# Three value projections in other column blocks, in a decoder of two blocks on one core

## The chip, the cores and the metric

The kernel runs on one core of one Trainium2 chip. The metric is the device time of one execution in microseconds (us), as the median over runs; lower is better.

The core has five engines that run side by side and meet through semaphores: TensorE (PE, matrix products into PSUM, with its weight loads listed apart as PEld), VectorE (DVE), ScalarE (ACT), GpSimd (POOL), and SyncE (SP), which here issues the loads of the weights. PSUM has eight banks of 512 fp32 columns.

## The reference, cut to what matters

Two models follow one another on a sequence of 256 tokens, model width 1024, all in fp32. The first has two layers: feed-forward, mixer, feed-forward; its mixers are a dilated attention and a retention. The second has two layers of a "mix" (differential attention, latent attention and attention to a memory, gated and summed) and an MLP. The three projections that the change touches:

```python
def retention(h, w_in, w_out, decay_logit):
    proj = (h @ w_in).astype(jnp.float32)
    dq = H_R * DK_R                                   # 1024
    q = proj[..., :dq].reshape(B, S, H_R, DK_R)
    k = proj[..., dq:2 * dq].reshape(B, S, H_R, DK_R)
    v = proj[..., 2 * dq:2 * dq + D_V]                # D_V = 2048: the retention's values
    ...
    q = rotary(q, pos)
    k = rotary(k, pos) * (DK_R ** -0.5)

# second block, for each of two layers; IN_SIZES = (1024, 1024, 1024, 384, 288, 512, 3072)
dq, dk, dv, c_q, c_kv_kr, xq, gate_logits = jnp.split(h @ w_in[l], split_idx, axis=-1)
y_diff = diff_attention(dq, dk, dv, ...) @ w_diff_o[l]   # q and k: rmsnorm per head, then rotary
```

`v` (2048 columns) and, twice, `dv` (1024 columns) are the value projections in question. Each is a product of a 256 x 1024 activation with a 1024 x n weight.

## The kernel before, in words

**Products in three passes.** fp32 products are made from a rounded high part and the rest: w = w_hi + w_lo, x = x_hi + x_lo, and x_hi w_hi + x_hi w_lo + x_lo w_hi are summed in one PSUM bank. The activation is stationary (128 tokens x 128 of the 1024 inputs), the weights stream. `pe_program`, step "mm" (lines 1929 to 1943), does for each half of the tokens and each chunk of 128 inputs three matmuls (L1936, L1937, L1938), as wide as the column block.

**Blocks and tiles.** `column_blocks` cuts n columns into blocks of BLOCK = 512. `project` (L668) goes through the blocks and calls `block`, which cuts the 8 chunks of inputs into tiles of weights: a tile holds TILE // n chunks (TILE = 1024), so 2 chunks at 512 columns, and 4 tiles make a block. At the last tile of a block two evacuation steps are emitted (one for each half of the tokens), that bring the bank to SBUF. `by_turns` gives each to ACT or to DVE, in a turn of four; the transposes of heads and the copies of transposed probabilities draw from the same turn.

**A tile's way.** SP loads it to one of four `w_raw` buffers, ACT rounds it to `w_hi` (L2228), DVE (or in some stages POOL for every second tile) subtracts to get `w_lo` (L2550, L3300), both in four buffers, and PE uses it. The split of tile i + 4 is emitted when tile i has been used (`tile_used`); the load of a tile waits for the `w_lo` of the tile four earlier. So PE has at most four split tiles ahead.

**The order.** One plan lists all steps, and each engine takes its own in that order. `drive(main, side)` runs the projections as `main` and lets `side` emit its steps after each tile, before `tile_used` emits the split:

```python
        self.step(kind, used)        # in tile(): PE's matmuls of this tile
        ...
            yield                    # side steps are emitted here
            self.tile_used(used)     # then the split of tile used + 4
```

In the retention (L1363 on), `qkv` projects q, k and v in this order, and `rotations` goes on by one step for each tile: tables for the decays, then for q two rotations ("turning", one for each half of the tokens, six DVE instructions each, L3148 to L3156) and four pairs of transposed heads (PE L2051), then the same for k. The gates' projections and the heads follow.

In a mix layer (L1577 on), `projections` goes through cq, ckv, q, k, v, then the two products of the latent attention, xq, and the gates. Beside them `in_step` runs, for each tile, `outputs` (the attention) once and the preparing generators three times; these normalise k straight from its banks (squares on ACT, powers on POOL, L3107 on DVE), rotate it (DVE L3148 to L3156) and transpose it four tiles later. `outputs` waits until q and k are transposed and all of v is there.

Of the kernel before, what the change touches and what calls it, by code (L numbers as in the profile page):

```python
# [19 lines left out]
D = 1024  # L20
# [18 lines left out]
H_R, DK_R, DV_R = 4, 256, 512  # L39
# [8 lines left out]
BLOCK = 512  # L48
# [8 lines left out]
IN_SIZES = dict(dq=1024, dk=1024, dv=1024, cq=MLA_QL, ckv=MLA_KVL + MLA_ROPE, xq=CROSS_H * CROSS_D, gate=3 * D)  # L57
IN_AT = dict(zip(IN_SIZES, np.cumsum([0] + list(IN_SIZES.values()))[:-1].tolist()))
# [55 lines left out]
TWO_PI_PARTS = two_pi_parts()  # L114


def column_blocks(n, start=0):
    return [(start + c, min(BLOCK, n - c)) for c in range(0, n, BLOCK)]


def spread(ap, dims):
# [283 lines left out]
class Kernel:  # L405
# [259 lines left out]
        self.flip = (self.flip + 1) % 4  # L665
        return "act" if self.flip < self.act_share else "dve"

    def project(self, xt, w, rows, n, dst, start=0, after=(), first=0):  # L668
        made = [[] for _ in range(HALVES)]
        for c0, m in column_blocks(n):  # L670

            def leave(b):
                for half in range(HALVES):
                    self.step("evac", Evac(b, half, self.by_turns(), dst[:, half, c0:c0 + m], list(after)))
                    made[half].append(("evac", b.uid, half))

            yield from self.block(xt, w, rows, start + c0, m, first, then=leave)
        return made
# [180 lines left out]
    def last_normed(self, xt, w, rows, factor, turned=None, rows_out=False):  # L859
# [14 lines left out]
        for c, (c0, m) in enumerate(column_blocks(D)):  # L874
            if c == 1 and not turned:
                self.hold_last(rows * BLOCK // (P * TILE))
            b = both if turned else (yield from self.block(xt, w, rows, c0, m))
            for half in range(HALVES):
                name = ("blk", b.uid, half, c) if turned else ("blk", b.uid, half)
                self.step("out_squares", st, half, c, name, sums[half][:, c:c + 1])  # L880
                self.step("out_gain", st, half, c, name, g, self.tok_after[half])
                gained[half, c] = "out_gain", st, half, c
                if (half, c) == (0, 1):
                    scale(0)
# [472 lines left out]
    def retention(self, i, j):  # L1357
# [3 lines left out]
        v = self.put("re_v", 32, [P, HALVES, H_R * DV_R])  # L1361
# [9 lines left out]
        w_in, got = a["ret_w_in"][0], {}  # L1371
# [4 lines left out]
        def qkv():  # L1376
            bs = yield from self.pair_of_blocks(self.xt, (w_in, 0), (w_in, BLOCK))
            got["q"] = [[] for _ in range(HALVES)]
            for c, b in enumerate(bs):
                for half in range(HALVES):  # L1380
                    self.step("evac", Evac(b, half, self.by_turns(), q[:, half, c * BLOCK:(c + 1) * BLOCK], []))
                    got["q"][half].append(("evac", b.uid, half))
            got["k"] = yield from self.project(self.xt, w_in, D, D, k, D)
            got["v"] = yield from self.project(self.xt, w_in, D, H_R * DV_R, v, 2 * D)

        def rotations():
            yield from self.decays()
            for name, z, zt, factor in (("q", q, qt, None), ("k", k, kt, DK_R ** -0.5)):
# [11 lines left out]
                yield  # L1400

        drive(qkv(), rotations())
        got["all"] = got["qt"] + got["kt"] + got["v"][0] + got["v"][1]
        self.ret_ready = got["all"]
# [156 lines left out]
    def mix(self, layer, _):  # L1561
# [3 lines left out]
        w_in = a["w_in_2"][layer]  # L1565
# [6 lines left out]
        v = self.put("mx_v" + L, 32, [P, HALVES, D])  # L1572
# [18 lines left out]
        got, mem_over, scaled = {}, [], dict(diff=[], mla=[], cross=[])  # L1591
# [8 lines left out]
        self.feed(memory_kv)  # L1600

        def projections():
            part = lambda name, dst, after=(): self.project(self.xt, w_in, D, IN_SIZES[name], dst, IN_AT[name], after)
            got["cq"] = yield from part("cq", low[:, :, 0:MLA_QL], self.tok_after[0])
            got["ckv"] = yield from part("ckv", low[:, :, CKV_AT:D], self.tok_after[0])
            got["q"] = yield from part("dq", q)
            for c0, m in column_blocks(D):
                got["k", c0] = yield from self.block(self.xt, w_in, D, IN_AT["dk"] + c0, m)
            got["v"] = yield from part("dv", v)
            yield from need("low_t", "ckt")  # L1610
            got["mq"] = yield from self.project(low_t, a["w_mla_qb_2"][layer], MLA_QL, MLA_H * MLA_QK, mq)
            got["kv"] = yield from self.project(low_t, a["w_mla_kvb_2"][layer], MLA_KVL, MLA_H * PER_KV, kv, first=MLA_QL // P)
            got["low", "over"] = self.last_tile()
            got["xq"] = yield from part("xq", xq, [got["low", "over"]])
            yield from need("qt")
            yield from gate(0)
            yield from need("kt")
            yield from gate(1)
            yield from need("cqt", "mkt")
            yield from gate(2)  # L1620
            self.xt_after = [self.last_tile()]
            yield from merge(0, 0, diff_t, "w_diff_o_2", D, 0)
            got["diff", "over"] = self.last_tile()
            yield from merge(1, 2, mc_t, "w_cross_o_2", CROSS_H * CROSS_D, 4)
            yield from merge(2, 1, mc_t, "w_mla_o_2", MLA_H * MLA_V, 0)

        def gate(g):
            gi = self.next_gain()
            for c0, m in column_blocks(D):
                b = yield from self.block(self.xt, w_in, D, IN_AT["gate"] + g * D + c0, m)  # L1630
                for half in range(HALVES):
                    self.step("gate_bias", layer, g, half, c0, gates[g][:, half, c0:c0 + m], b, gi)
            self.step("next_gain", gi + 2, [("gate_bias", layer, g, HALVES - 1, D - BLOCK)])
# [3 lines left out]
        def merge(n, g, xt, name, rows, first):  # L1637
            while any((int(xt is mc_t), first + i) not in turned_out for i in range(rows // P)):
                yield IDLE
            for half in range(HALVES):  # L1640
                self.step("sigmoid", layer, g, half, gates[g][:, half, :])
            view, nk = a[name][layer].rearrange("(k p) n -> p k n", p=P), TILE // BLOCK
            for c, (c0, m) in enumerate(column_blocks(D)):
                b = self.new_block(xt, first, rows // P, m)
                tiles = [Tile(view[:, k0:k0 + nk, c0:c0 + m], nk, m, b, k0) for k0 in range(0, rows // P, nk)]
                for t in tiles[:-1]:
                    yield from self.tile(t, "mm")
                self.tiles.append(tiles[-1])
                used = len(self.tiles) - 1
                done = lambda half: self.step("merge", layer, n, half, c, b, merged[:, half, c0:c0 + m], gates[g][:, half, c0:c0 + m], g)  # L1650
                if n == 2 and c == 1:
                    self.step("mm", used, 0)
                    last_half.update(used=used, merge=done)
                    return
                self.step("mm", used)
                yield
                for half in range(HALVES):
                    done(half)
                self.split(used + SPLIT)
# [5 lines left out]
        def need(*names):  # L1665
            while any(name not in got for name in names):
                yield IDLE
# [156 lines left out]
        prepared = together(memory_keys(), diff_keys(), diff_queries(), latent(), latent_keys(), cross_queries(), diff_outputs())  # L1824
        side = self.in_step(prepared, outputs())
        drive(projections(), side, finish=False)
        merged_t = self.put_t("mx_merged_t" + L, 32, DC)

# [1627 lines left out]
```

## Time and profile before

| | us |
|---|---|
| median of three runs | 2375.38 |
| lowest, highest | 2372.74, 2375.89 |
| the profiled execution's own time | 2375.64 |
| its span, first to last instruction | 2374.3 |

| engine | busy us | share of the span |
|---|---|---|
| PE | 2337.1 | 98% |
| PEld | 1931.7 | 81% |
| DVE | 1579.3 | 67% |
| ACT | 1232.3 | 52% |
| POOL | 283.5 | 12% |

The mean granted clock of TensorE is 0.998 of full speed. The profile is one execution. Matmuls are pipelined: a listed duration holds the time from start to the modelled end and overlaps the next one's, so the pace is read from starts. In a timeline, columns are start in us from the span's start, duration in us, engine, line, operation, outputs<-inputs, shape and count; neighbours of one kind may be merged, and idle time before an instruction stands in brackets with what ended it.

### The profile page before, as it was taken

The numbers are of one execution on the slowest core, as the hardware profiler recorded it, in microseconds if no ns is written. First come the engines' busy times: TensorE is split into PE (matmuls) and PEld (weight loads), VectorE is DVE, ScalarE is ACT, GpSimd is POOL, SyncE is SP. The second block draws the span as 40 slices with busy tenths as digits, with TensorE's granted clock in tenths as the row PEclk, the third lists the DMA queues.
The fourth block names the chain that finished last, engine by engine and source line by source line (L and its number), as shares of the span: only waits on it lengthen the run. The fifth ranks groups of instructions, "written<-read, shape, count | busy, mean of one in ns | idle before, by whom it ended". The sixth has DMA issues, their size and how long they took to land.

```text
span 2374.3 us, 31048 instructions
## 1 busy us (share of the span) xinstructions
PE 2337.1 (98%) x12268; PEld 1931.7 (81%) x12268; DVE 1579.3 (67%) x2409; ACT 1232.3 (52%) x1942; POOL 283.5 (12%) x247
## 2 busy tenths in 40 slices
PE   9999999999999999999999999999999999999999
PEld 7887788778878877777788887788888887888887
DVE  6765566777656757666676677755775687656764
ACT  5554454455545536444555565555554555554643
POOL 1100010000000000000001121434110122433000
PEclk9999999999999999999999999999999999999999
DMA  7765544455665656544567654435666554345564
GB/s 229 207 202 173 169 127 136 151 186 178 195 193 180 189 185 199 172 135 151 185 189 215 192 180 142 124 126 185 187 200 208 185 167 131 119 143 173 186 193 144
DMA packets 263265, 411.44 MB, mean 173 GB/s; under 512 B 13770, under 2 KB 129370, under 8 KB 263120
## 3 DMA queue, kind: packets, MB, share of 16 engines
q1 hardware_dynamic: 256256, 389.59, 52.1%
q0 software_dynamic: 6432, 19.28, 3.2%
q8 instruction: 97, 1.59, 0.3%
q10 hardware_dynamic: 432, 0.59, 0.1%
q14 instruction: 48, 0.39, 0.1%
HBM read 408.31 MB, written 1.10 MB: 172 GB/s over the span
## 4 chain that ended last, share of the span: by engine, by line
PE 84%; DVE 10%; ACT 4%; issue 1%; POOL 1%; DMA 0%; ACTq 0%; DVEq 0%
PE banks L1936 16%; PE banks L1938 16%; PE banks L1937 16%; PE banks L1964 15%; PE banks L1965 8%; DVE w_lo L2550 3%; ACT w_hi L2228 2%; PE banks L2038 1%; PE banks L2098 1%; PE banks L2051 1%; DVE probs L2772 1%; PE banks L1919 1%; PE banks L1925 1%; PE banks L1920 1%; PE banks L2083 1%
## 5 line engine op out<-in xcount | busy, mean ns | idle before, releaser
L2550 DVE TENSOR_TENSOR w_lo<-w_raw,w_hi 128x1024 fp32r<-128x1024 f32 x688 | 836.5, 1224 | 536.2 <-ACT w_hi L2228 527.9
L2228 ACT ACTIVATE w_hi<-w_raw 128x1024 fp32r<-128x1024 f32 (+2 forms) x744 | 775.3, 1049 | 450.6 <-PE banks L1938 370.6
L1964 PE MATMUL banks<-xt,w_hi 128*128 128x512 f32 x1632 | 572.9, 394 | 1.2 <-DVE w_lo L2550 1.2
L1965 PE MATMUL banks<-xt,w_lo 128*128 128x256 f32 x1632 | 455.4, 279 | 0.0
L1936 PE MATMUL banks<-w_hi,xt 128*128 128x512 f32 (+2 forms) x1056 | 432.8, 410 | 7.0 <-DVE xt L2578 3.6
L1938 PE MATMUL banks<-w_hi,xt 128*128 128x512 f32 (+2 forms) x1056 | 414.1, 392 | 0.0
L1937 PE MATMUL banks<-w_lo,xt 128*128 128x512 f32 (+2 forms) x1056 | 413.0, 391 | 0.0
L1964 PEld LDWEIGHTS banks<-xt,w_hi 128*128 128x128 f32 x1632 | 305.8, 187 | 75.2 <-issue 2.6
L1965 PEld LDWEIGHTS banks<-xt,w_lo 128*128 128x128 f32 x1632 | 305.8, 187 | 0.0
L1936 PEld LDWEIGHTS banks<-w_hi,xt 128*128 128x128 f32 x1056 | 199.3, 189 | 52.5 <-DVE w_lo L2550 9.0
L1938 PEld LDWEIGHTS banks<-w_hi,xt 128*128 128x128 f32 x1056 | 199.2, 189 | 45.4
L1937 PEld LDWEIGHTS banks<-w_lo,xt 128*128 128x128 f32 x1056 | 199.9, 189 | 42.0 <-issue 3.1
L3281 POOL TENSOR_TENSOR stat<-stat,minus_half 128x1 f32<-128x1 f32 (+2 forms) x60 | 56.3, 943 | 1024.6 <-DVE stat L2538 549.7
L3300 POOL TENSOR_TENSOR w_lo<-w_raw,w_hi 128x1024 fp32r<-128x1024 f32 x56 | 134.4, 2400 | 263.9 <-ACT w_hi L2228 263.8
L1936 PE MATMUL banks<-w_hi,ffn_ht_hi 128*128 128x512 f32 x320 | 127.9, 400 | 0.0
L1938 PE MATMUL banks<-w_hi,ffn_ht_lo 128*128 128x512 f32 x320 | 126.1, 394 | 0.0
L1937 PE MATMUL banks<-w_lo,ffn_ht_hi 128*128 128x512 f32 x320 | 125.5, 392 | 0.0
L1938 PE MATMUL banks<-w_hi,mlp_ht_lo 128*128 128x512 f32 x256 | 101.7, 397 | 0.0
L1937 PE MATMUL banks<-w_lo,mlp_ht_hi 128*128 128x512 f32 x256 | 101.1, 395 | 0.0
L1936 PE MATMUL banks<-w_hi,mlp_ht_hi 128*128 128x512 f32 x256 | 100.8, 394 | 0.0
L2355 ACT ACTIVATE probs<-probs,mx_nmax 128x256 f32<-128x256 f32 x96 | 42.9, 448 | 81.9 <-DVE mx_nmax L2772 81.9
L2695 DVE TENSOR_TENSOR tmp<-banks,tmp 128x256 f32<-128x256 f32 x204 | 76.4, 417 | 0.0
(447 smaller groups left out, 3155.9 us busy)
## 6 DMA issues: line engine op xcount, KB each, us to landing
w_raw<-in_w_mlp SPq DMA_DIRECT2D x128, 512.0 KB, 4.0
w_raw<-in_w_in SPq DMA_DIRECT2D x104, 512.0 KB, 3.6
w_raw<-in_ffn_w_gate SPq DMA_DIRECT2D x88, 512.0 KB, 4.2
w_raw<-in_ffn_w_up SPq DMA_DIRECT2D x88, 512.0 KB, 4.5
w_raw<-in_ffn_w_down SPq DMA_DIRECT2D x88, 512.0 KB, 4.0
w_raw<-in_attn_w_in SPq DMA_DIRECT2D x72, 512.0 KB, 3.5
w_raw<-in_ret_w_in SPq DMA_DIRECT2D x64, 512.0 KB, 4.0
w_raw<-in_ret_w_out SPq DMA_DIRECT2D x16, 512.0 KB, 3.3
```

The lines of the kernel that those rows point to most:

```text
L1919: pe.matmul(bank, xh, hi[:, j * t.n:(j + 1) * t.n], start=(c == 0), stop=False)
L1936: pe.matmul(bank, xh, wh, start=(c == 0), stop=False)
L1937: pe.matmul(bank, xh, wl, start=False, stop=False)
L1938: mm = pe.matmul(bank, xl, wh, start=False, stop=(c == b.chunks - 1))
L1964: pe.matmul(pair, hi[:, cols], both, start=(c == 0), stop=False)
L1965: mm = pe.matmul(out[f], lo[:, cols], xh, start=False, stop=(c == DC - 1))
L2228: act.activation(k.w_hi[i % SPLIT][:, 0:m], k.raw[i % RAW][:, 0:m], ACT.Copy).then_inc(*ev.mark(k.w_hi_made, ("w_hi", i)))
L2355: act.activation(row, row, ACT.Exp, bias=h.nmax[:, s:s + 1], scale=-1.0, accum_out=h.den[:, s:s + 1]).then_inc(*done)
L2550: dve.tensor_tensor(lo, raw, hi.bitcast(F32), ALU.subtract).then_inc(*ev.mark(k.w_lo_made, ("w_lo", i)))
L2695: dve.tensor_tensor(part, bank[:, 0:SEQ], part, ALU.add).then_inc(*ev.mark(k.dve_done, ("hid_joined", *name, f), ("bank", "blk", b.uid, f)))
L3281: pool.tensor_tensor(out, mean, k.minus_half[:, 0:n], ALU.pow).then_inc(*ev.mark(k.pool_done, name))
L3300: pool.tensor_tensor(lo, raw, hi.bitcast(F32), ALU.subtract).then_inc(*ev.mark(k.w_lo_pool, ("w_lo", i)))
```

## The change

`column_blocks` gets a list of widths in place of its unused `start`, `project` passes it on, and three calls name widths. All else (the step's order by tile, the buffers, the turn of the engines) stays as it is in the code.

```diff
-def column_blocks(n, start=0):
-    return [(start + c, min(BLOCK, n - c)) for c in range(0, n, BLOCK)]
+def column_blocks(n, widths=()):
+    if widths:
+        assert sum(widths) == n
+        return [(sum(widths[:i]), m) for i, m in enumerate(widths)]
+    return [(c, min(BLOCK, n - c)) for c in range(0, n, BLOCK)]
...
-    def project(self, xt, w, rows, n, dst, start=0, after=(), first=0):
+    def project(self, xt, w, rows, n, dst, start=0, after=(), first=0, widths=()):
         made = [[] for _ in range(HALVES)]
-        for c0, m in column_blocks(n):
+        for c0, m in column_blocks(n, widths):
...
-            got["v"] = yield from self.project(self.xt, w_in, D, H_R * DV_R, v, 2 * D)
+            got["v"] = yield from self.project(self.xt, w_in, D, H_R * DV_R, v, 2 * D, widths=(416, 416, 416, 416, 384))
...
-            part = lambda name, dst, after=(): self.project(self.xt, w_in, D, IN_SIZES[name], dst, IN_AT[name], after)
+            part = lambda name, dst, after=(), widths=(): self.project(self.xt, w_in, D, IN_SIZES[name], dst, IN_AT[name], after, widths=widths)
...
-            got["v"] = yield from part("dv", v)
+            got["v"] = yield from part("dv", v, widths=((448, 288, 288), (480, 272, 272))[layer])
```

By TILE // n a block of 416, 384, 448 or 480 columns still has 4 tiles of 2 chunks (832, 768, 896, 960 columns in the tile). A block of 288 or 272 has three tiles, of 3, 3 and 2 chunks (864, 864, 576, or 816, 816, 544). The retention's values go from 4 blocks and 16 tiles to 5 and 20; each mixer's from 2 blocks and 8 tiles to 3 and 10.

## Rows read from the trace of the kernel before

**Rows 1.** The page, its first part: engine, busy us, share of the span, instructions.

```profile
PE 2337.1 (98%) x12268; PEld 1931.7 (81%) x12268; DVE 1579.3 (67%) x2409; ACT 1232.3 (52%) x1942; POOL 283.5 (12%) x247
```

**Rows 2.** Busy time by stretch: the values of the retention and of the first mixer.

```profile
core 0: us, PE busy (x) PEld busy (x) DVE busy (x) ACT busy (x) POOL busy (x), PEclk, DMA share, GB/s
930.70:979.10 48.40, 48.40 (x225) 39.21 (x224) 39.31 (x49) 21.57 (x24) 0.00 (x0) 1.00 0.60 185
1426.00:1451.50 25.50, 24.46 (x115) 19.63 (x114) 21.34 (x30) 12.41 (x16) 3.33 (x2) 1.00 0.52 165
```

**Rows 3.** PE's waits, whole span: waiting line, releaser, us in total, times, longest.

```profile
PE banks L2083 <- ACT probs L2355: 7.9, 13, 1.4
...
PE banks L1936 <- DVE w_lo L2550: 2.1, 2, 1.0
```

**Rows 4.** Timeline of PE, first mix layer: ends of runs of equal matmuls.

```profile
1362.56 0.34 PE L1936 MATMUL banks<-w_hi,xt 128*128 128x384 f32 x1
...
1370.87 0.29 PE L1936 MATMUL banks<-w_hi,xt 128*128 128x288 f32 x1
...
1375.67 1.04 PE L2051 MATMUL banks<-ident,mx_ck 128*128 128x128 f32 x8
...
1404.54 0.40 PE L1936 MATMUL banks<-w_hi,xt 128*128 128x512 f32 x1
...
1418.36 0.39 PE L1938 MATMUL banks<-w_hi,xt 128*128 128x512 f32 x1
```

**Rows 5.** DVE by line and shape: count, busy us, mean ns, idle before.

```profile
L2550 DVE TENSOR_TENSOR w_lo<-w_raw,w_hi 128x1024 fp32r<-128x1024 f32 x670 | 820.4, 1232 | 525.6 <-ACT w_hi L2228 517.3
...
L2550 DVE TENSOR_TENSOR w_lo<-w_raw,w_hi 128x864 fp32r<-128x864 f32 x4 | 4.2, 1050 | 0.0
L2550 DVE TENSOR_TENSOR w_lo<-w_raw,w_hi 128x576 fp32r<-128x576 f32 x2 | 1.5, 752 | 0.0
```

**Rows 6.** Timeline of PE, retention: start of the values, first transposes of q.

```profile
930.70 0.40 PE L1936 MATMUL banks<-w_hi,xt 128*128 128x512 f32 x1
...
941.94 0.60 PE L2051 MATMUL banks<-ident,re_q 128*128 128x128 f32 x4
```

**Rows 7.** Timeline of DVE, retention: starts of q's two rotations and of splits.

```profile
932.40 0.68 DVE L3148 TENSOR_TENSOR tmp<-re_q,re_rope 128x512 f32<-128x512 f32 x1
...
936.13 1.22 DVE L2550 TENSOR_TENSOR w_lo<-w_raw,w_hi 128x1024 fp32r<-128x1024 f32 x1
937.27 0.69 DVE L3148 TENSOR_TENSOR tmp<-re_q,re_rope 128x512 f32<-128x512 f32 x1
...
941.01 2.36 DVE L2550 TENSOR_TENSOR w_lo<-w_raw,w_hi 128x1024 fp32r<-128x1024 f32 x2
```

**Rows 8.** Timelines, retention: PE at the ninth value tile, DVE at k's rotations.

```profile
954.99 0.40 PE L1936 MATMUL banks<-w_hi,xt 128*128 128x512 f32 x1
...
958.00 0.68 DVE L3148 TENSOR_TENSOR tmp<-re_k,re_rope 128x512 f32<-128x512 f32 x1
...
961.74 1.22 DVE L2550 TENSOR_TENSOR w_lo<-w_raw,w_hi 128x1024 fp32r<-128x1024 f32 x1
```

**Rows 9.** Timeline of PE, first mixer: the first and the seventh value tile.

```profile
1425.99 0.48 PE L1936 MATMUL banks<-w_hi,xt 128*128 128x512 f32 x1
...
1444.14 0.50 PE L1936 MATMUL banks<-w_hi,xt 128*128 128x512 f32 x1 [1.04 <-DVE w_lo L2550]
```

**Rows 10.** Timeline of DVE, first mixer: k's first rotation, the splits behind both.

```profile
1434.25 0.69 DVE L3148 TENSOR_TENSOR tmp<-mx_k,rope_k 128x512 f32<-128x512 f32 x1
...
1437.99 1.22 DVE L2550 TENSOR_TENSOR w_lo<-w_raw,w_hi 128x1024 fp32r<-128x1024 f32 x1
...
1442.87 2.35 DVE L2550 TENSOR_TENSOR w_lo<-w_raw,w_hi 128x1024 fp32r<-128x1024 f32 x2
```

**Rows 11.** Timelines, second mixer: start of the values, k's first rotation.

```profile
1943.30 0.48 PE L1936 MATMUL banks<-w_hi,xt 128*128 128x512 f32 x1
...
1951.55 0.69 DVE L3148 TENSOR_TENSOR tmp<-mx_k,rope_k 128x512 f32<-128x512 f32 x1
```

**Rows 12.** Timeline of ACT, retention: a tile's w_hi that waited for its load.

```profile
946.96 1.06 ACT L2228 ACTIVATE w_hi<-w_raw 128x1024 fp32r<-128x1024 f32 x1 [0.48 <-DMA w_raw<-in_ret_w_in]
```

## The prediction

> **What bounds the kernel now.** I read the page first: TensorE (PE) is busy for 98% of the span [rows 1], so the question is what the change does to PE's own work and to its waits. Then the stretches table for two of the three value projections: 48.4 us in the retention, PE without idle time, and 25.5 us in the first mixer, PE idle for 1.04 us; the granted clock is 1.00, the 2.4 GHz level, and VectorE (DVE) is busy for 39.3 of 48.4 and 21.3 of 25.5 us [rows 2]. Then the waits: PE's L1936 waited for DVE's w_lo twice, 1.0 us each, and those are in the mixers' value projections; the largest other entry is the attention's wait for ScalarE (ACT), 7.9 us in 13 [rows 3]. Last the timelines, for the pace of PE and for what DVE does meanwhile. So PE sets the time, and DVE, which splits each weight tile (L2550) and also does the rotations, stands close behind it in just these stretches.
>
> **PE's work.** A matmul's listed duration overlaps its neighbour's, so I take starts. 60 matmuls of 512 columns: first start 1404.54, last 1418.36, 59 intervals, 0.2342 us each. 48 of 384 columns from 1362.56 to 1370.87: 0.1731. 36 of 288 from 1370.87 to 1375.67: 0.1333 [rows 4]. At 2.4 columns per ns these are 213.3, 160.0 and 120.0 ns of streaming, so what comes on top is 20.9 ns at 512, 13.1 at 384 and 13.3 at 288. For 272 I take 13.3: 0.1267. For 416, 448 and 480 no row exists: below, 13.3 on top (0.1867, 0.2000, 0.2133), above, 20.9 as at 512 (0.1942, 0.2076, 0.2209). I take the lower, since the two measured widths under 512 agree, and keep the upper.
> - Retention: 4 blocks x 8 chunks x 2 halves x 3 = 192 matmuls at 0.2342 = 44.97 us. After: 4 x 48 = 192 at 0.1867 and 48 at 0.1731 = 44.16. -0.8 us (upper end +0.6).
> - Each mixer: 96 at 0.2342 = 22.48. After, first: 48 at 0.2000 + 96 at 0.1333 = 22.40; second: 48 at 0.2133 + 96 at 0.1267 = 22.40. -0.1 each (upper end +0.3 each).
> Sum -1.0 us, upper end +1.2. There are 144 more matmuls, but less is paid on top of each.
>
> The rows show 13 to 21 ns on top of the streaming [rows 4]. The Trainium skill, "TensorE: Matmul & The Clock Gate", section "Back-to-back issue gap", gives N/2.4 + 2.5 ns, the same amount at every width. By it 144 more matmuls would add 0.4 us instead of taking 1.0 away. The trace does not agree with the 2.5 ns at any width, so the rows decide.
>
> **DVE and ACT.** A split of 1024 columns costs DVE 1.232 us, of 864 1.050, of 576 0.752 [rows 5]; that is about 1.08 ns a column and 0.12 us fixed. 832 comes to 1.02, 896 to 1.09, 960 to 1.16, 816 to 1.00, 544 to 0.71. The columns are the same in sum; 4 + 2 + 2 more tiles add 8 x 0.12 = 1 us on DVE over 99 us in which it has some 17 us free: nothing by itself. The evacuations grow from 8 to 10 and from 4 to 6, also off the path. What matters is *when* a split comes.
>
> **The new wait.** The side work goes on by tiles: after tile n of a projection the same step is emitted as before. A rotation is six DVE instructions, about 3.73 us in a row, and the splits stand behind it in DVE's queue. Its start depends on data (evacuations, POOL's powers), not on how fast PE goes through the tiles. PE lives on four split tiles ahead; a tile was 12 x 0.2342 = 2.81 us of PE and is now 12 x 0.1867 = 2.24 in the retention, 2.40 in the first mixer, 2.56 then 2.28 in the second (18 x 0.1267). The cover shrinks, the rotations don't. I number value tiles v0, v1, ...
>
> Retention, q's rotations. v0 starts at 930.70 and the first transposes of q come after v3, at 941.94 [rows 6]. DVE rotates from 932.40 to 936.13, splits v3, rotates from 937.27 to 941.01, and the next split is v4's, done 1.22 later, 0.15 us before PE took it [rows 7]. After: DVE starts 0.2 sooner (narrower split ahead), ends the first rotation at 935.93, split pitch 0.94, second ends at 940.6; v4's split is done at 941.65. PE ends v3 at 930.70 + 4 x 2.24 = 939.66, waits for the rotation until 940.7, transposes (0.43), waits for v4 until 941.65. Without waits it would be at 940.1: **+1.6 us**.
> Retention, k's rotations. From the start of v8 (954.99) to that of the first rotation (958.00) are 3.0 us [rows 8], evacuation, w_hi and w_lo; narrower 2.55. After: v4 at 941.65, v5 to v7 with transposes, v8 at 952.0; rotations 954.6 to 958.3 and 959.3 to 963.0, v13's split done at 964.0. PE has v12 done at 963.2, transposes to 963.7: **+0.3**.
>
> First mixer. v0 starts at 1425.99, v6 at 1444.14 after the wait of 1.04; without it at 1442.94 [rows 9], so 1.2 us are lost already. DVE rotates from 1434.25, again until 1442.87, and only then splits v6 [rows 10]. After: rotations start about 0.25 us sooner (two narrower splits ahead). First ends 1437.7, v5's split (864) 1438.8, second ends 1442.4, v6's split (576) 1443.2. PE would take v5 at 1425.99 + 0.07 + 5 x 2.40 = 1438.06 and waits 0.7; done 1441.2, then waits 2.0 for v6. 2.7 against 1.2 before: **+1.5**. Behind it DVE catches up.
> Second mixer. v0 at 1943.30, rotation at 1951.55 [rows 11]. After: rotations from 1951.4, v5's split 1956.2, v6's 1960.55. PE wants v5 at 1943.30 + 0.07 + 4 x 2.56 + 2.28 = 1955.9 (waits 0.3, done 1958.5) and v6 (waits 2.1): 2.4 against 1.2: **+1.2**.
> Waits in sum +4.6 (lower end 0 if the rotations move with PE, and -2.4 if even the two old waits go). These stretches are not covered by anything: PE is the path.
>
> **Transfers.** A tile shrinks from 512 KB, its rows from 2048 to between 1088 and 1920 bytes. In the retention's stretch ACT waited for w_raw once, 0.48 us, for v8 at 946.96 [rows 12]; PE took v8 at 954.99, 8.0 us later, of which w_hi and w_lo need 2.3. Cost nothing; at the upper end 1 us if rows this short land late. The attention behind the mixers' projections starts after the same tile as before (it needs all of v). Two more evacuations move on the turn of ACT and DVE by two: before the first mixer's v (the retention's shift), and behind the second's. Two evacuations change engine in places where PE waits for ACT up to 1.4 us [rows 3]; I take 0 and keep +/-1.4.
>
> **Sum.** -1.0 + 4.6 = +3.6 us. The profiled execution took 2375.64 us with a span of 2374.3; its 2375.64 + 3.6 = 2379.2. The median of the runs shown is 2375.38, 0.3 below; I name 2379.0. A measurement of this kernel tells about 0.2% (4.75 us) from no change, so the likeliest case lies inside that.
>
> **Rivals.**
> 1. *The rotations keep pace with PE.* Where their start hangs on slots that PE frees (k in the retention partly does), the waits stay as they were: -1.0, 2374.4. For it: ACT and DVE spend much time waiting for PE. Against: in [rows 7, 10] they start on q's and k's last banks, done before the narrow tiles begin. Chance 0.22.
> 2. *Faster: the old waits go.* In both mixers v6 is only 576 or 544 wide, its split 0.5 us shorter; if the rotations also came one tile later for PE (v7), DVE would be ahead by a tile and 2 x 1.2 us would be won: -3.4, 2372.0. It decides in favour if v6's split is done before 1442.9; my count has 1443.2. Against: the step's tile is fixed by counting. Chance 0.08.
> 3. *Slower: the extra 7.6 ns belong to all widths over 384.* PE's work is then +1.2 instead of -1.0, and the waits shrink by about 0.8 since tiles are longer: +5.0, 2380.4. Decides where 416's interval is over 0.190 us. Chance 0.15.
> 4. *Slower: the evacuations' turn in the second mixer's attention* adds waits for ACT there, some +2 to +3 on the sum: 2381.5. Chance 0.07.
> 5. *The fixed-gap rule of above as the whole story:* matmuls +0.4, otherwise as forecast: +5.0, near rival 3; no row bears it out. Chance 0.01.
> The forecast has 0.47, its own range 2377 to 2381.
>
> Range 2373.5 to 2382.5. Faster by over 0.2%: 0.06 (part of rival 2, and what I overlook). Slower by over 0.2%: 0.26 (most of rivals 3 to 5, the upper part of the forecast). Within: 0.68.
>
> **What would show it.** Starts of 416-column matmuls 0.187 apart (rival 3: 0.194), 448 0.200, 480 0.213. PE's waits for w_lo in the v stretches: none in the retention before, now one at v4 with a wait of the transposes for re_q just ahead; in each mixer two, at v5 (0.7 and 0.3) and v6 (2.0 and 2.1). The stretches: 48.4 becomes about 49.5, 25.5 becomes 26.9 and 26.7. No growth of ACT's waits for w_raw. It is wrong if the rotations start more than 1 us sooner, if PE's wait at v6 shrinks, or if the time moves outside these three stretches.

## The result, and the profile after

The changed kernel took 2380.7 us (median of ten runs, 2379.33 to 2382.73), the kernel before 2374.76 us (median of ten on the same chip, 2372.74 to 2376.32): ratio 1.0026, 95% interval 1.0016 to 1.0035. The forecast was 2379.0, in a range of 2373.5 to 2382.5, with no measurable change (within 0.2%) as the likeliest outcome. The time lies 1.7 us over the forecast and the ratio just over 0.2%, with 0.2% inside its interval.

The profiled execution of the changed kernel took 2379.33 us, with a span of 2378.0: 3.7 us more than before. I cut both spans where the value projections' first matmul and the first matmul behind them start, in us:

| stretch | before | after | difference | forecast |
|---|---|---|---|---|
| all before the retention's values | 930.70 | 929.20 | -1.50 | 0 |
| the retention's values | 48.42 | 49.52 | +1.10 | +1.1 |
| up to the first mixer's values | 446.88 | 446.81 | -0.07 | 0 |
| the first mixer's values | 25.53 | 27.02 | +1.49 | +1.4 |
| first mixer, the 40 tiles behind | 170.83 | 170.74 | -0.09 | 0 |
| up to the second mixer's values | 320.94 | 320.97 | +0.03 | 0 |
| the second mixer's values | 25.54 | 26.60 | +1.06 | +1.1 |
| second mixer, the 40 tiles behind | 170.84 | 172.48 | +1.64 | 0 |
| the rest | 234.64 | 234.66 | +0.02 | 0 |

The three stretches of the change sum to +3.65. Something outside them adds 1.64, and the start hides 1.50 of it. The start is chance: in the thirteen profiled executions of this study, all with the same work up to there, it took from 929.20 to 931.63 us. The 1.50 between these two profiles lie almost wholly at one place. In twelve of the thirteen executions the granted clock (last column but two) fell to the 1.2 GHz level near 211 us, where PE has two waits of 1.3 us; the first profile of the changed kernel is the one in which it held. Before, then after:

```profile
212.00:215.00 3.00, 3.00 (x9) 2.32 (x8) 2.93 (x5) 0.00 (x0) 0.17 (x1) 0.50 0.00 0
212.00:215.00 3.00, 3.00 (x18) 2.50 (x17) 2.93 (x5) 0.08 (x1) 0.05 (x1) 1.00 0.00 0
```

Without the start the change costs +5.2 us, and +5.5 in a second profile of the changed kernel (its span of 2380.7 less 931.63, against 2374.3 less 930.70). The difference of the medians is 5.9.

The engines' line of the page, after, answers to [rows 1]: PE has 144 instructions more and 3 us less of listed work, and everything that was added is idle time.

```profile
PE 2334.0 (98%) x12412; PEld 1944.0 (82%) x12412; DVE 1582.0 (67%) x2419; ACT 1234.5 (52%) x1954; POOL 284.0 (12%) x247
```

The same columns as in [rows 2], after, for the three stretches. The clock is 1.00 as before, while PE is now idle for 0.9, 2.3 and 1.8 us (before: 0, 1.0 and 1.0).

```profile
929.20:978.70 49.50, 48.62 (x273) 47.29 (x272) 39.84 (x54) 23.57 (x30) 0.00 (x0) 1.00 0.59 180
1425.50:1452.50 27.00, 24.72 (x163) 23.65 (x162) 21.64 (x32) 13.15 (x19) 3.24 (x2) 1.00 0.54 154
1944.20:1970.90 26.70, 24.87 (x164) 23.09 (x163) 21.55 (x32) 13.66 (x20) 3.24 (x2) 1.00 0.53 152
```

PE's waits over the whole span, after. L1939 is what L1936 was, L2086 what L2083 was. Against [rows 3], both lines have grown: the attention's wait for ACT by 1.5 us, the projections' wait for the splits from 2 times to 5.

```profile
PE banks L2086 <- ACT probs L2358: 9.4, 13, 1.6
PE banks L1939 <- DVE w_lo L2553: 4.6, 5, 1.8
```

PE in the retention's values, after, starts of v0, v3, q's first transposes, v4, v8, v12 and v13. The tiles v8 to v11 take 9.01 us in 48 matmuls of 416 columns: 0.1877 each. The two waits of the forecast stand at v4 and v13, with the transposes' own wait for `re_q` ahead of v4.

```profile
929.20 0.35 PE L1939 MATMUL banks<-w_hi,xt 128*128 128x416 f32 x1
...
935.96 0.35 PE L1939 MATMUL banks<-w_hi,xt 128*128 128x416 f32 x1
...
938.77 0.63 PE L2054 MATMUL banks<-ident,re_q 128*128 128x128 f32 x4 [0.39 <-DVE re_q L3159]
939.71 0.42 PE L1939 MATMUL banks<-w_hi,xt 128*128 128x416 f32 x1 [0.31 <-DVE w_lo L2553]
...
950.14 0.35 PE L1939 MATMUL banks<-w_hi,xt 128*128 128x416 f32 x1
...
959.15 0.35 PE L1939 MATMUL banks<-w_hi,xt 128*128 128x416 f32 x1
...
962.19 0.46 PE L1939 MATMUL banks<-w_hi,xt 128*128 128x416 f32 x1 [0.18 <-DVE w_lo L2553]
```

DVE there, after, answers to [rows 7]: the first rotation starts 0.94 us behind v0 (it was 1.70), and the split of v4 is the first of three merged behind the second rotation.

```profile
930.14 0.68 DVE L3151 TENSOR_TENSOR tmp<-re_q,re_rope 128x512 f32<-128x512 f32 x1
...
938.54 2.89 DVE L2553 TENSOR_TENSOR w_lo<-w_raw,w_hi 128x832 fp32r<-128x832 f32 x3
```

PE in the first mixer's values, after, answers to [rows 9]: v0, v1, v4, v5 and v6. v1 to v3 take 7.20 us in 36 matmuls, 0.2000 each, and v5 and v6 both wait.

```profile
1425.52 0.45 PE L1939 MATMUL banks<-w_hi,xt 128*128 128x448 f32 x1
...
1428.02 0.36 PE L1939 MATMUL banks<-w_hi,xt 128*128 128x448 f32 x1
...
1435.22 0.29 PE L1939 MATMUL banks<-w_hi,xt 128*128 128x288 f32 x1
...
1438.30 0.40 PE L1939 MATMUL banks<-w_hi,xt 128*128 128x288 f32 x1 [0.53 <-DVE w_lo L2553]
...
1442.70 0.40 PE L1939 MATMUL banks<-w_hi,xt 128*128 128x288 f32 x1 [1.75 <-DVE w_lo L2553]
```

DVE there, after, answers to [rows 10]. The rotation starts 7.93 us behind v0 (it was 8.26). The split of v6 ends at 1442.65, and PE takes v6 at 1442.70.

```profile
1433.45 0.69 DVE L3151 TENSOR_TENSOR tmp<-mx_k,rope_k 128x512 f32<-128x512 f32 x1
...
1437.19 1.05 DVE L2553 TENSOR_TENSOR w_lo<-w_raw,w_hi 128x864 fp32r<-128x864 f32 x1
...
1441.90 0.75 DVE L2553 TENSOR_TENSOR w_lo<-w_raw,w_hi 128x576 fp32r<-128x576 f32 x1
```

PE in the second mixer's values, after: v0, v1, the last matmul of 480 columns, v4, v5, v6. From v1's start to that last one are 7.66 us in 35 intervals, 0.2189 each. Here v5 doesn't wait.

```profile
1944.25 0.47 PE L1939 MATMUL banks<-w_hi,xt 128*128 128x480 f32 x1
...
1946.97 0.38 PE L1939 MATMUL banks<-w_hi,xt 128*128 128x480 f32 x1
...
1954.63 0.38 PE L1941 MATMUL banks<-w_hi,xt 128*128 128x480 f32 x1
1954.85 0.29 PE L1939 MATMUL banks<-w_hi,xt 128*128 128x272 f32 x1
...
1957.10 0.40 PE L1939 MATMUL banks<-w_hi,xt 128*128 128x272 f32 x1
...
1961.47 0.39 PE L1939 MATMUL banks<-w_hi,xt 128*128 128x272 f32 x1 [1.83 <-DVE w_lo L2553]
```

The second mixer's attention, 1970.8 to 2073 us, after: PE's largest wait, and the copies of transposed probabilities by engine and shape. Before, the same wait (1968.8 to 2070) summed to 3.5 us, and ACT did 12 of these 18 copies (10 of 384 columns, 2 of 512) and DVE 6. Now it is 15 and 3. The wait before, then after:

```profile
PE banks L2083 <- ACT probs L2355: 3.5, 6, 1.4
```

```profile
PE banks L2086 <- ACT probs L2358: 5.0, 6, 1.6
```

The copies before, then after:

```profile
L2375 ACT ACTIVATE probs_t<-banks 128x384 f32<-128x384 f32 x10 | 4.7, 470 | 0.0
...
L2791 DVE COPY probs_t<-banks 128x384 f32<-128x384 f32 x6 | 3.3, 555 | 2.3 <-PE banks L2083 2.3
```

```profile
L2378 ACT ACTIVATE probs_t<-banks 128x384 f32<-128x384 f32 x14 | 6.6, 471 | 1.0 <-PE banks L2086 1.0
...
L2794 DVE COPY probs_t<-banks 128x384 f32<-128x384 f32 x2 | 1.1, 554 | 0.0
L2794 DVE COPY probs_t<-banks 128x512 f32<-128x512 f32 x1 | 0.7, 683 | 0.0
...
L2378 ACT ACTIVATE probs_t<-banks 128x512 f32<-128x512 f32 x1 | 0.6, 599 | 0.0
```

### The profile page after: what moved, and what is told of

It reads as the page before. It is cut to its first block, busy times and chain, and to the rows that moved or that the text cites. A ratio compares the mean times of both kernels' runs of the same rounds, so it can differ in the third digit from the quotient of the medians.

```text
span 2378.0 us, 31372 instructions
## 1 busy us (share of the span) xinstructions
PE 2334.0 (98%) x12412; PEld 1944.0 (82%) x12412; DVE 1582.0 (67%) x2419; ACT 1234.5 (52%) x1954; POOL 284.0 (12%) x247
## 4 chain that ended last, share of the span: by engine, by line
PE 82%; DVE 11%; ACT 5%; issue 1%; POOL 1%; DMA 0%; SPq 0%; ACTq 0%; DVEq 0%
PE banks L1939 16%; PE banks L1941 16%; PE banks L1940 15%; PE banks L1967 15%; PE banks L1968 8%; DVE w_lo L2553 3%; ACT w_hi L2231 2%; PE banks L2041 1%; PE banks L2101 1%; PE banks L2054 1%; DVE probs L2775 1%; PE banks L1922 1%; ACT probs L2358 1%; PE banks L1923 1%; PE banks L1928 1%
## 5 line engine op out<-in xcount | busy, mean ns | idle before, releaser
L2553 DVE TENSOR_TENSOR w_lo<-w_raw,w_hi 128x1024 fp32r<-128x1024 f32 (+5 forms) x696 | 837.9, 1212 | 545.4 <-ACT w_hi L2231 536.9
L2231 ACT ACTIVATE w_hi<-w_raw 128x1024 fp32r<-128x1024 f32 (+4 forms) x752 | 777.0, 1040 | 456.4 <-PE banks L1941 366.4
L1939 PE MATMUL banks<-w_hi,xt 128*128 128x512 f32 (+6 forms) x1104 | 440.2, 399 | 9.5 <-DVE w_lo L2553 4.6
L1941 PE MATMUL banks<-w_hi,xt 128*128 128x512 f32 (+6 forms) x1104 | 421.1, 381 | 0.0
L1940 PE MATMUL banks<-w_lo,xt 128*128 128x512 f32 (+6 forms) x1104 | 420.1, 381 | 0.0
L1939 PEld LDWEIGHTS banks<-w_hi,xt 128*128 128x128 f32 x1104 | 207.9, 188 | 50.6 <-DVE w_lo L2553 11.3
L1941 PEld LDWEIGHTS banks<-w_hi,xt 128*128 128x128 f32 x1104 | 207.8, 188 | 40.2
L1940 PEld LDWEIGHTS banks<-w_lo,xt 128*128 128x128 f32 x1104 | 208.5, 189 | 37.4 <-issue 3.1
L1939 PE MATMUL banks<-w_hi,ffn_ht_hi 128*128 128x512 f32 x320 | 127.9, 400 | 0.0
L1939 PE MATMUL banks<-w_hi,mlp_ht_hi 128*128 128x512 f32 x256 | 100.8, 394 | 0.0
```

The costliest lines, as they stand in the source:

```text
L1939: pe.matmul(bank, xh, wh, start=(c == 0), stop=False)
L1940: pe.matmul(bank, xh, wl, start=False, stop=False)
L1941: mm = pe.matmul(bank, xl, wh, start=False, stop=(c == b.chunks - 1))
L2231: act.activation(k.w_hi[i % SPLIT][:, 0:m], k.raw[i % RAW][:, 0:m], ACT.Copy).then_inc(*ev.mark(k.w_hi_made, ("w_hi", i)))
L2553: dve.tensor_tensor(lo, raw, hi.bitcast(F32), ALU.subtract).then_inc(*ev.mark(k.w_lo_made, ("w_lo", i)))
```

## Experiments

The first four take the change apart: widths in the retention, widths in the mixers, and the turn by which evacuations and copies go to ACT or DVE. The turn (`flip`) counts them modulo four: two of its values give the step to ACT, two to DVE. Each longer list has one block more, so two evacuations more, and moves the turn by two. In the changed kernel the retention's shift and the first mixer's cancel, so the turn is as before behind the first mixer's values and is moved by two behind the second's. "Giving the turn back" undoes the shift:

```diff
+        if widths:
+            self.flip = (self.flip + 2) % 4    # at the end of project()
```

**e1_ret**: the retention's widths alone, the mixers' calls as before, the turn given back.

> Only the retention's values in 416 (384) columns; the turn of ACT and DVE is given back afterwards (flip moved on by two), so that every later evacuation falls to the same engine as before. Theory (DVE's rotations outlast the four tiles of cover): the stretch of the retention's values 48.4 becomes 49.5 us, with waits at v4 and v13, nothing else moves, total +1.1. Rival (the narrow blocks cost by themselves, in matmuls or in transfers): the stretch grows without waits for w_lo or for the rotations. Rival (all 5.9 us come from the three stretches): +1.6 to +2.

2376.46 us (11 runs) against 2375.4 (33 runs): 1.0004 (0.9995 to 1.0013). The retention's stretch is 49.55, every stretch behind it is within 0.04 us of before, and PE's waits are the same three as after. The retention costs 1.1 us.

**e2_mix**: the mixers' widths alone, the turn given back.

> Only the two mixers' values in 448 + 288 + 288 and 480 + 272 + 272 columns, turn given back after each. Theory: the stretches 25.5 and 25.5 become 27.0 and 26.6 us with waits for w_lo at v5 and v6; the second mixer's attention stays as before; total +2.6. Rival (the attention suffers from the extra tiles and not from the turn): a further +1.9 in the second mixer's attention, total +4.5.

2379.38 us (11 runs): 1.0016 (1.0007 to 1.0025), 4.0 us over the kernel before where 2.6 were expected. The second mixer's attention is 170.74, so the additional tiles cost nothing there and that rival falls. The second mixer's stretch is 26.60, as after. The first took 28.60 instead of 27.02, with the same wait at v6. Granted clock (the last column but two) in the first mixer, three stretches of e2_mix around the start of v6 at 1442.92:

```profile
1438.00:1442.90 4.90, 2.66 (x18) 2.43 (x18) 4.87 (x9) 1.61 (x2) 0.00 (x0) 1.00 0.23 60
1442.90:1443.90 1.00, 0.98 (x6) 0.98 (x7) 1.00 (x2) 0.00 (x0) 0.00 (x0) 0.78 0.00 0
1443.90:1446.10 2.20, 2.20 (x11) 2.18 (x11) 2.00 (x3) 0.33 (x1) 0.00 (x0) 0.50 0.88 264
```

The clock fell to the 1.2 GHz level (0.50) behind v6's start and was back at 1.00 by 1447. There, matmuls of 288 columns start 0.240 us apart instead of 0.133, and twelve transposes took 2.14 us instead of 1.47. That is the 1.6 us by which the stretch is longer. The runs that were not profiled differ too: the mean clock on record is 0.997 in six of the eleven, as in this profile, and 0.998 or 0.999 in the other five.

**e3_all_turn**: all widths, the turn given back.

> The whole change with the turn given back after each of the three projections. Theory: +1.1 + 1.5 + 1.1 = +3.7, the attention behind the second mixer's values as before the change (PE waits for ACT's probs there 3.5 us). Rival (turn has no part): +5.5, with 5.0 us of those waits.

2378.21 us (11 runs): 1.0012 (1.0003 to 1.0021). The three stretches are 49.55, 27.01 and 26.61, and the second attention is 170.75, as before the change. Its wait at v6 was as long as e2_mix's (1.74 us), but the clock held:

```profile
1443.70:1446.10 2.40, 2.40 (x22) 2.40 (x22) 2.18 (x4) 1.45 (x3) 0.00 (x0) 1.00 0.87 282
```

**e4_turn_only**: the kernel before, and behind the second mixer's values the turn moved on by two. No width is changed.

```diff
             got["v"] = yield from part("dv", v)
+            if layer == 1:
+                self.flip = (self.flip + 2) % 4
```

> The kernel before, all blocks 512 wide; only the turn of ACT and DVE is moved on by two behind the second mixer's values. Theory: +1.85, all of it in that mixer's attention, PE's waits for ACT's probs there from 3.5 to about 5.0 us. Rival (the turn has no part): 0.

2377.18 us (11 runs): 1.0008 (0.9999 to 1.0017). All stretches are as before but the second attention, 172.59 (+1.75), with the same wait as after, on the same waiting step:

```profile
PE banks L2085 <- ACT probs L2357: 5.0, 6, 1.6
```

Its copies are split 15 to 3 too. So the 1.64 us outside the three stretches are the turn's, and the parts add up: 1.1 + 1.5 + 1.06 + 1.75 = 5.4, where the changed kernel's two profiles gave 5.2 and 5.5.

**e5_narrow_first**: e2_mix with the narrow blocks ahead of the wide one.

```diff
-widths=((448, 288, 288), (480, 272, 272))[layer])
+widths=((288, 288, 448), (272, 272, 480))[layer])
```

> Only the mixers' values, narrow blocks first: 288 + 288 + 448 and 272 + 272 + 480, turn given back. Same matmuls, same splits, same number of tiles as in 448 + 288 + 288; only the work that PE has left before v5 and v6 is less. Theory (cover): v5 and v6 wait longer; stretches 28.7 and 29.5 us instead of 27.0 and 26.6, total +7.2 against the kernel before. Rival (what is paid is paid for each block or tile, or for narrow matmuls): same stretches as with the wide block first, total +2.6.

2385.01 us (4 runs) against 2375.05 (16 runs): 1.0044 (1.0031 to 1.0058). The stretches are 30.44 and 31.07. The waits for splits over the whole span were 4.1 us in 3 in e2_mix and are now

```profile
PE banks L1941 <- DVE w_lo L2555: 8.5, 4, 3.1
```

so the cover shrinks as forecast when the thin tile v5 stands between the rotations. On top, the clock fell in both mixers (0.79 over 1442 to 1450, 0.69 over 1965 to 1969). The excess over the forecast, 1.7 and 1.6 us, is about what the fall cost in e2_mix.

**e6_all_pool**: e3_all_turn, with the splits that stand between and behind the rotations (retention v3, v4, v12, v13; each mixer v5, v6) on POOL.

```diff
-        self.step("split", i, "pool" if self.share and i % self.share == 0 else "dve")
+        self.step("split", i, "pool" if self.share and i % self.share == 0 or i in self.on_pool else "dve")
```

> The whole change, turn given back, and the splits that stand between and behind the rotations given to POOL instead of DVE: v3, v4, v12, v13 in the retention, v5, v6 in each mixer. Theory: PE no longer waits for w_lo; retention 49.5 to about 47.9, mixers 27.0 and 26.6 to 24.3 and 24.1 us; total -3.1 against the kernel before. Rival (POOL's splits, twice as long, slow DVE's rotations or come late): the stretches shrink by less than half of that.

2381.14 us (6 runs): 1.003 (1.0018 to 1.0042). The expectation failed: retention 53.59, mixers 25.96 and 25.53. Against e3_all_turn both mixers still won 1.1 us, and the retention lost 4.0. In the retention, POOL, then DVE in the same moment:

```profile
932.32 4.71 POOL L3309 TENSOR_TENSOR w_lo<-w_raw,w_hi 128x832 fp32r<-128x832 f32 x2 [31.28 <-ACT w_hi L2237]
```

```profile
932.82 2.37 DVE L3160 TENSOR_TENSOR re_q<-re_q,re_rope 128x512 f32<-128x512 f32 x1
935.11 2.48 DVE L3161 TENSOR_TENSOR re_q<-re_q,re_rope 128x512 f32<-128x512 f32 x1
```

Two instructions of 0.69 us took 2.4 each while POOL split two tiles. PE no longer waits for a split in the retention, but for what the rotation makes; in the mixers it waits for the rotated `mx_k` in the same way, 1.5 and 1.0 us.

```profile
PE banks L2060 <- DVE re_q L3165: 2.9, 1, 2.9
PE banks L2060 <- DVE re_k L3165: 2.3, 1, 2.3
```

**e7_before_pool**: the kernel before (512 columns everywhere), the splits of v5 and v6 of each mixer on POOL, by the same edit.

> The kernel before (512 columns) with only the splits of v5 and v6 in each mixer given to POOL. Theory: the two old waits of 1.2 us go, stretches 25.5 to 24.3 us each, total -2.4. Rival (as above): less than half of it.

2372.66 us (11 runs) against 2375.05: 0.9989 (0.998 to 0.9998), lower than both kernels. Both mixers' stretches are 24.22 (-1.31 each), and PE has no wait for DVE's splits there. POOL and DVE in the first mixer:

```profile
1433.75 2.39 POOL L3302 TENSOR_TENSOR w_lo<-w_raw,w_hi 128x1024 fp32r<-128x1024 f32 x1
1436.38 2.57 POOL L3302 TENSOR_TENSOR w_lo<-w_raw,w_hi 128x1024 fp32r<-128x1024 f32 x1 [0.24 <-ACT w_hi L2230]
```

```profile
1433.88 0.75 DVE L3109 SCALAR_TENSOR_TENSOR mx_k<-banks,row_scale,stat 128x512 f32<-128x512 f32 x1 [0.94 <-POOL stat L3283]
1434.74 1.96 DVE L3150 TENSOR_TENSOR tmp<-mx_k,rope_k 128x512 f32<-128x512 f32 x1
1436.61 2.89 DVE L3151 TENSOR_TENSOR tmp<-mx_k,rope_k 128x512 f32<-128x512 f32 x1
```

DVE is held here as well, but nothing that PE needs soon is behind it: both splits in question are POOL's, and the transposes come four tiles later.

**e8_pace**: e2_mix with 464 + 280 + 280 and 496 + 264 + 264, for the matmul's interval at four more widths.

> Only the mixers' values, in 464 + 280 + 280 and 496 + 264 + 264 columns, turn given back: one look, for the interval of matmuls of further widths. If the larger extra begins between 448 and 480: 464 gives 193.3 + 13.5 = 206.8 ns or 193.3 + 18 = 211.6; 496 gives 206.7 + 19 to 21 = 226 to 228 ns. 264 and 280 columns: 110 + 13.3 = 123.3 and 116.7 + 13.3 = 130.0 ns.

2378.89 us (one run), stretches 28.39 (a fall of the clock to 0.50 in the first mixer again) and 26.40. Mean interval, from starts in the traces of this kernel, of the changed one and of the one before, without the first interval of a mixer's values, which is some 90 ns longer:

| columns | 264 | 272 | 280 | 288 | 384 | 416 | 448 | 464 | 480 | 496 | 512 |
|---|---|---|---|---|---|---|---|---|---|---|---|
| interval, ns | 121.6 | 125.4 | 129.6 | 133.1 | 173.4 | 187.7 | 200.2 | 210.2 | 218.9 | 225.2 | 234.2 |
| on top of columns / 2.4 | 11.6 | 12.1 | 12.9 | 13.1 | 13.4 | 14.4 | 13.5 | 16.9 | 18.9 | 18.5 | 20.9 |

What comes on top lies between 11.6 and 14.4 ns up to 448 columns and rises from there to 20.9 at 512.

**e9_mix_again** and **e10_after_again**: e2_mix and the changed kernel once more, unchanged, to see whether the fall belongs to the program.

> The narrow columns in both mixers alone, once more (v's turn given back), for what the granted clock does behind the wait at v6 of the first mixer. Theory: the fall to the 1.2 GHz level for some 2.4 us is not fixed by the program; it comes in some executions and costs 1.6 us. Then this execution may show either: first mixer's stretch 28.6 us (fall) or 27.0 us (no fall), second 26.6, span 2378.0 or 2376.4. Rival: the fall belongs to this program (to where its wait starts against the work before): 28.6 again. A stretch of 27.0 refutes the rival; 28.6 leaves both.

2379.05 us (one run). The first mixer took 27.03, the clock at 1.00 throughout, and the second 28.17, with the fall there. The rival is refuted: of two executions of one program one fell in the first mixer alone and the other in the second alone. The two ran on different chips, so this pair alone can't tell a chip's part from an execution's. But the eleven runs of e2_mix were on one chip, and their mean clocks differ. e9_mix_again in the second mixer, v6 starting at 1961.39 behind its wait:

```profile
1962.00:1964.00 2.00, 2.00 (x10) 2.00 (x10) 2.00 (x4) 0.12 (x1) 0.00 (x0) 0.50 0.71 164
```

> The changed kernel once more, as it is, for the same question. Theory: the stretch of the first mixer's values is 27.0 us as in its first profile if the clock holds, 28.6 if it falls behind v6's wait; retention 49.5, second mixer 26.6 (28.2 with a fall), second attention 172.5; span 2378.0 or up to 2381. Rival: the changed kernel never falls there, and the scatter of its spans (2378.0 to 2381.4) comes from the start of the kernel alone: 27.0 and 26.6, and any difference of the span lies in the first 929 us.

2381.99 us (one run), stretches 49.54, 27.04, 26.61 and 172.57: no fall in these stretches. Of the 2.7 us more of span than in the first profile, 2.43 lie ahead of the retention's values, 1.5 of them in the fall near 211 us that the first profile lacks. The executions of kernels with all widths (the changed one twice, e3_all_turn) show no fall in six mixers, those with the mixers' alone (e2_mix, e9_mix_again, e8_pace, e5_narrow_first) five in eight. That doesn't show the changed kernel to be free of it: two of its ten runs, 2382.66 and 2382.73 us, the slowest, have a mean clock of 0.997, as the profile of e2_mix with its fall has. Of 64 runs of the kernel before, one has it. No trace shows where those two fell.

**e11_one_pool**: e7_before_pool with v6 alone on POOL.

```diff
-            self.on_pool |= {len(self.tiles) + 5, len(self.tiles) + 6}
+            self.on_pool |= {len(self.tiles) + 6}
```

> The kernel before with one split of each mixer's values, v6's, on POOL, v5's left on DVE. Theory (PE waits because v6's split stands behind two rotations in DVE's queue; POOL's read and write hold DVE's rotation while they overlap): v6's w_lo is there before PE needs it, the wait of 1.0 us goes in both mixers, the stretches are 24.2 each as with two splits on POOL, and since DVE is held only once, some 2.4 us instead of 4, nothing is late behind it: 2374.8 - 2.6 = 2372.2. Rival: DVE, held by POOL and with v5's split of 1.2 us still in its queue, is late for v7 (it was 2.35 us for two splits behind the rotations): PE waits there some 0.5 to 1.5 us instead, stretches 24.8 to 25.7, 2373.3 to 2375.

2376.67 us (11 runs) against 2375.0 (15 runs): 1.0007 (0.9998 to 1.0016), stretches 25.66 and 25.68. The theory failed, and so did the rival's place: the wait came to v5, not v7. POOL, DVE and PE of the first mixer:

```profile
1435.09 2.63 POOL L3302 TENSOR_TENSOR w_lo<-w_raw,w_hi 128x1024 fp32r<-128x1024 f32 x1 [2.61 <-ACT w_hi L2230]
```

```profile
1435.38 2.88 DVE L3154 TENSOR_TENSOR mx_k<-mx_k,rope_k 128x512 f32<-128x512 f32 x1
...
1439.39 1.21 DVE L2552 TENSOR_TENSOR w_lo<-w_raw,w_hi 128x1024 fp32r<-128x1024 f32 x1
```

```profile
1440.66 0.50 PE L1938 MATMUL banks<-w_hi,xt 128*128 128x512 f32 x1 [1.19 <-DVE w_lo L2552]
```

The held rotation pushed v5's split to 1440.60, and PE wanted it at 1439.3. It is the same wait, one tile earlier. The stretches account for 0.3 us over the kernel before; the medians differ by 1.7, and no trace shows the rest. The interval of the ratio holds both. With both splits on POOL nothing that PE needs soon is left behind the rotation, which is why e7 wins.

## Why the prediction came out as it did

- **The mechanism and its sum held for the three stretches.** +3.6 was forecast for them, +3.65 came. Waits stand at the tiles named: v4 and v13 of the retention, v5 and v6 of the first mixer, v6 of the second.
- **PE's work**: -1.0 forecast. From the intervals above, the retention gave -0.6 (16 tiles of 2.25 and 4 of 2.08 us against 16 of 2.81), the first mixer -0.1. The second gave +0.1: 48 x 0.2189 + 96 x 0.1254 = 22.55 against 22.48, since 480 columns have 18.9 ns on top and not 13.3. So -0.6 in sum. Taking the lower bound was right for 416 and 448; for 480 the truth lies nearer the upper one. Rival 3 (20.9 ns for all widths over 384) fell with 416's 0.1877.
- **Retention, q: +1.6 forecast, +1.06 measured** (v3 took 3.74 us; 2.25 of matmuls and the 0.43 of its transposes leave 1.06). The rotation started 0.8 us sooner against v0 than before, not 0.2: the forecast counted one narrower split ahead of it, and there were three (v0's to v2's). So v4's split was done 10.36 us behind v0 and not 10.95. k: +0.3 forecast, +0.36 measured. What the wait lacked, the matmuls and the transposes had more, so the stretch's 49.5 was right with terms half a microsecond off.
- **First mixer: +1.5 forecast.** v5 starts 0.7 and v6 2.0 later than the pace alone would have it (forecast 0.7 and 2.0), against 1.2 before. Splits were done 12.72 and 17.13 us behind v0 (forecast 12.81 and 17.21).
- **Second mixer: +1.2 forecast.** v6 lost 2.1 as forecast. v5 lost nothing, not 0.3, because the four tiles of 480 took 0.3 us longer. The error in the work and the one in the wait are the same quantity seen twice: while DVE sets the time, a slower PE costs nothing.
- **The mis-sized step is the turn of ACT and DVE**, "I take 0 and keep +/-1.4". It cost 1.64 to 1.75 us, which e4_turn_only shows without any change of widths. Three more of the 18 copies went to ACT, the engine for which PE waits there. The prediction had named time outside the three stretches as a sign of being wrong, and it came. Rival 4 had the place right, and asked 2 to 3. The 2380.7 measured equals the forecast plus this term, 2379.0 + 1.7, but that it fits so closely is luck: the median of the kernel before came out 0.6 us lower than the one forecast from, and the medians differ by 0.5 us more than the parts add up to. That the time fell inside the range, with a term of 1.7 us taken as 0, owes something to the range's width.
- **"No growth of ACT's waits for w_raw" was wrong**: in the retention they went from 0.5 us in one to 2.6 in two (longest 1.4), and in the mixers, where there were none, to 3.1 us in one and 1.7 in one. It cost nothing, as forecast: in the retention every tile but v3, v4, v12 and v13 was split at least 1.8 us ahead of PE, in the mixers every tile behind v6 at least 1.4 us.
- **Rivals 1 and 2** (rotations keep pace, old waits go) fell with the rows of DVE: k's in the retention moved with PE, as the forecast had it, but q's there and the mixers' started only 0.2 to 0.8 us sooner against v0, while PE would have reached the tile behind them 2.2, 2.0 and 1.3 us sooner. Rival 5 fell with the intervals.

The chances left 0.26 for slower by over 0.2%, and the measured ratio lies at that edge.

## What to carry to other kernels

When one engine runs a fixed number of tiles ahead of another, narrower tiles shorten the cover in time, while the block of other work between the tiles (here 3.7 us of rotation) stays as long. Compare the block with the cover before touching the widths. Look for everything that counts blocks, too: a turn that picks an engine is moved by them, far behind the edit, and that was a third of the cost here. And before a step goes to an idle engine, see what the two hold in common.

## What the runs showed of the hardware

- **POOL's split holds DVE's instructions with two SBUF operands.** In the stretches of e6_all_pool, e7_before_pool and e11_one_pool POOL did 14 splits. Each time a DVE instruction of 0.69 us began beside the split and ended 0.54 to 0.56 us behind its end, for example 935.19 against 934.63 in e6_all_pool, 1436.70 against 1436.14 in e7_before_pool, 1438.26 against 1437.72 in e11_one_pool. L3109, which reads a PSUM bank, took its usual 0.75 us beside POOL's split. The trace of the kernel before has it already, in the mixers' merges: six of L3269's instructions began beside a split of POOL and took 2.03 to 2.08 us, the ten others 0.69. The Trainium skill, "SBUF — State Buffer", section "SBUF: two separate sides", says it of such pairs: whichever starts first has the shared port pair for its whole instruction, and the other is blocked. The runs agree, and by it, or by those rows, the failure of e6_all_pool could have been foreseen.
- **A wait of under 2 us can bring TensorE to 1.2 GHz, in some executions.** In e2_mix the granted clock was 1.00 up to the end of the wait and fell about 0.5 us after work had begun again; the price was 1.6 us there, nearly as much as the wait itself, and 1.4 to 1.7 us in all five falls. Those are five of eight mixers in kernels with the mixers' widths alone, at waits of 1.7 to 3.1 us. None of eight did in the traces of the kernel before, e1_ret, e4_turn_only and e11_one_pool, with waits of 1.0 to 1.2 us. Yet near 211 us twelve of thirteen executions fell, at two waits of 1.3 us that end 2.0 us apart. What decides between executions of one program is open.
- **A matmul's interval on top of its columns isn't one number**: 11.6 ns at 264 columns, 13.1 to 14.4 from 288 to 448, 20.9 at 512.
